# Matmuls of z for two groups at once in a two-layer hybrid encoder

## What is computed

```
proj = x @ w_in[i]                 # GLU input | two branch gates | z (2048) | xBC (4096) | dt
A:  u = a * sigmoid(gt); u = depthwise_conv(u, 31 taps); u = silu(layer_norm(u)); y_a = u @ w_a_out
B:  xbc = silu(depthwise_conv(xBC, 5 taps)) -> xs (2048), B, C (8 groups of 128 each)
    y = ssd_forward + ssd_backward + xs * d_skip          # chunks of 128 tokens
    y = y * silu(z); y = y / rms(y within a group of 256) * norm_g; y_b = y @ w_b_out
merged = sigmoid(gate_A) * y_a + sigmoid(gate_B) * y_b
h  = layer_norm(alpha * x + merged @ w_o)
h2 = layer_norm(alpha * h + swiglu(h))
x  = h2 + rms_norm(p @ w_ple) * sigmoid(h2 @ w_ple_gate)
```

## Time and profile before

| | |
|---|---|
| runs | 2437.61, 2442.34 (median), 2445.15 us |
| profiled execution | 2438.85 us, span of its trace 2437.2 us |
| granted clock of TensorE | 0.996 of full speed |
| DMA moved | 406 MB, mean 167 GB/s |
| chain that ended last | PE 84%, ACT 4%, DVE 4%, DMA 3%, issue 3% |

### The profile page before, as it was taken

How to read it: one execution, slowest core, us unless ns; L and a number is a source line. 1 busy time by engine, 2 the same in 40 slices (tenths; PEclk the granted TensorE clock), 3 DMA queues, 4 the chain that set the end, 5 groups by cost and what they waited for, 6 DMA issues and landing times.

```text
span 2437.2 us, 35277 instructions
## 1 busy us (share of the span) xinstructions
PE 2380.4 (98%) x11464; PEld 1944.8 (80%) x11464; DVE 1486.2 (61%) x2553; ACT 1370.6 (56%) x2238; POOL 585.9 (24%) x721
## 2 busy tenths in 40 slices
PE   8999999999999999999999999999999999999998
PEld 6878788887777888887778787888878778888876
DVE  5899999989546111113659989989895451111136
ACT  6755666475564644345567466665746555444455
POOL 3423333242111111111134243332411111111110
PEclk9999999999999999999999999999999999999999
DMA  8576574756787788899664756747577868888884
GB/s 214 125 171 141 132 184 112 162 139 155 173 185 186 165 194 193 188 197 201 160 160 107 183 122 157 164 115 174 119 175 171 204 150 192 191 193 189 196 206 121
DMA packets 111172, 406.04 MB, mean 167 GB/s; under 512 B 12336, under 2 KB 12336, under 8 KB 110768
## 3 DMA queue, kind: packets, MB, share of 16 engines
q0 software_dynamic: 54144, 197.16, 47.4%
q1 hardware_dynamic: 55728, 202.66, 24.2%
q10 hardware_dynamic: 1152, 4.37, 0.5%
HBM read 402.04 MB, written 2.10 MB: 166 GB/s over the span
## 4 chain that ended last, share of the span: by engine, by line
PE 84%; ACT 4%; DVE 4%; DMA 3%; issue 3%; POOL 0%; ACTq 0%; SPq 0%; POOLq 0%; DVEq 0%; another core or an unknown queue 0%
PE bank L835 22%; PE bank L837 22%; PE bank L836 22%; PE bank L878 3%; PE bank L877 3%; PE bank L880 2%; DMA w_raw<-w_stream 2%; PE bank L951 2%; PE bank L957 1%; DMA w_lo<-w_stream 1%; ACT w_lo L465 1%; PE bank L939 1%; ACT w_hi L464 1%; PE bank L1156 1%; PE bank L922 1%
## 5 line engine op out<-in xcount | busy, mean ns | idle before, releaser
L352 POOL DMA_DIRECT2D w_lo<-w_stream x376 | 327.5, 871 | 1576.4 <-ACT w_lo L465 1525.4
L835 PE MATMUL bank<-x_hi,w_hi 128*128 128x512 f32 x1728 | 685.9, 397 | 4.6 <-DMA w_lo<-w_stream 4.6
L837 PE MATMUL bank<-x_hi,w_lo 128*128 128x512 f32 x1728 | 673.8, 390 | 0.0
L836 PE MATMUL bank<-x_lo,w_hi 128*128 128x512 f32 x1728 | 672.8, 389 | 0.0
L464 ACT ACTIVATE w_hi<-w_raw 128x1024 fp32r<-128x1024 f32 x378 | 402.7, 1065 | 287.2 <-PE bank L837 232.0
L465 ACT ACTIVATE w_lo<-w_raw 128x1024 fp32r<-128x1024 f32 x378 | 399.9, 1058 | 0.0
L835 PEld LDWEIGHTS bank<-x_hi,w_hi 128*128 128x128 f32 x1728 | 324.5, 188 | 74.7 <-issue 8.8
L837 PEld LDWEIGHTS bank<-x_hi,w_lo 128*128 128x128 f32 x1728 | 324.3, 188 | 69.0
L836 PEld LDWEIGHTS bank<-x_lo,w_hi 128*128 128x128 f32 x1728 | 324.6, 188 | 68.3 <-issue 3.3
L1238 DVE SCALAR_TENSOR_TENSOR z_a<-glu_out,params,z_a 128x497 f32<-128x497 f32 (+14 forms) x480 | 320.1, 737 | 0.0
L1685 DVE TENSOR_TENSOR glu_out<-bank,sigmoids 128x512 f32<-128x512 f32 x44 | 30.4, 692 | 416.5 <-PE bank L837 416.5
(11 more groups left out here) (242 smaller groups left out, 3611.2 us busy)
## 6 DMA issues: line engine op xcount, KB each, us to landing
w_raw<-w_stream SPq DMA_DIRECT2D x378, 512.0 KB, 4.5
w_lo<-w_stream POOLq DMA_DIRECT2D x376, 512.0 KB, 7.2
z_b<-x_in SPq DMA_DIRECT2D x4, 512.0 KB, 6.9
w_ple_in<-w_ple ACTq DMA_DIRECT2D x2, 1024.0 KB, 11.4
out<-z_b SPq DMA_DIRECT2D x4, 512.0 KB, 7.1
ple_p<-p_in ACTq DMA_DIRECT2D x2, 512.0 KB, 6.7
params<-par_in ACTq DMA_DIRECT2D x2, 340.0 KB, 3.8
tmp_m<-w_dt ACTq DMA_DIRECT2D x2, 256.0 KB, 5.2
```

Of the source, the lines that this page charges most:

```text
L352: gp.dma_start(wlo[:, s, :], w_stream[cyc, s].bitcast(F32R), accum_op=ALU.add).then_inc(lo_done[s], 16)
L835: pe.matmul(dst, wh, mh, start=first, stop=False)
L836: pe.matmul(dst, wh, ml, start=False, stop=False)
L837: return pe.matmul(dst, wl, mh, start=False, stop=last)
```

## The change

TensorE makes z of both groups of a pair together: the stationary operand stays a tile of x (128 features x 128 tokens), and the moving one is now 512 columns, z's filters of both groups for one tile of features. A slot holds two such tiles, so z takes four passes over the four banks (`z_pass`, one chunk of tokens per bank), of 24 matmuls each. The filter tiles of the second group's xs, xs and B come ahead of z in the stream, and its C behind. Results of z stay in the four banks until the fourth pass; then ScalarE's `z_gate` takes each chunk. With that:

- ScalarE's roundings (`hi`) and GpSimd's `lo` issues change places within the pair, and z_gate, the squares and the takes of the convolution input with them.
- ScalarE makes the middle tap of three of the four convolution calls of a pair and of the long convolution of branch A (`middle_tap`, `middle_tap_a`, Identity with scale and bias). VectorE's `taps` leaves it out there.
- The squares for the group norm write into z_tok in place of a tile of their own.
- Gate B's second cycle: its slot 0 is rounded among the squares of branch A, and its first two tiles are copied to glu_out and taken as sigmoids later.
- Gate of PLE: a slot is rounded ahead of the sigmoid instead of behind it. The square root of PLE's norm comes after the fifth rounding of the activations instead of the eighth.

```diff
@@ TensorE: z
-            def z_tiles(cyc, s, chunks=range(CH)):
...
-                    for k in range(KT):
-                        h, l, end = whi[:, s:s + 2, w], wlo[:, s:s + 2, w], k == KT - 1
-                        pe.matmul(dst, xh[:, k, t], h, start=k == 0, stop=False)
...
+            def z_pass(c0, n, chunks=range(CH), last=True):
+                cyc, s = on(c0, 1 if n == 0 else 2), (n - 1) % SLOTS
+                pe.wait_ge(lo_done[s], 16 * (cyc[0] + 1))
+                for i, c in enumerate(chunks):
+                    if n == 0:
+                        pe.wait_ge(evac[c], seen(c0[1] + (1 if c == CH - 1 else 2)))
+                    t = slice(c * P, (c + 1) * P)
+                    for k in (2 * n, 2 * n + 1):
+                        w = slice(k % 2 * T, (k % 2 + 1) * T)
+                        pe.matmul(bank[c][:, :], xh[:, k, t], whi[:, s, w], start=k == 0, stop=False)
+                        pe.matmul(bank[c][:, :], xh[:, k, t], wlo[:, s, w], start=False, stop=False)
+                        q = pe.matmul(bank[c][:, :], xl[:, k, t], whi[:, s, w], start=False, stop=k == KT - 1)
...
@@ TensorE: pair
-                z_tiles(on(c0, 1), 0)
-                dense(on(c0, 1), 2, xh, xl)
+                for n in range(3):
+                    dense(on(c0, 1), n, xh, xl)
                 xs_transpose(G0)
                 exponent(G0, 0, True)
-                dense(on(c0, 1), 3, xh, xl)
+                z_pass(c0, 0, (3, 0, 1, 2))
                 b_transpose(G0)
                 c_dot_b(G0)
                 exponent(G0, 1, True)
-                dense(on(c0, 2), 0, xh, xl)
+                z_pass(c0, 1, (0, 1), False)
+                state(G0, 0)
                 exponent(G0, 2)
-                state(G0, 0)
-                dense(on(c0, 2), 1, xh, xl)
+                z_pass(c0, 1, (2, 3))
                 exponent(G0, 3)
                 state(G0, 1)
                 state(G0, 2)
-                z_tiles(on(c0, 2), 2, (0, 1))
+                z_pass(c0, 2)
+                z_pass(c0, 3, (0, 1), False)
                 y_chunk(G0, 0)
-                z_tiles(on(c0, 2), 2, (2,))
+                z_pass(c0, 3, (2,), False)
                 y_chunk(G0, 1)
                 y_chunk(G0, 2)
-                z_tiles(on(c0, 2), 2, (3,))
+                z_pass(c0, 3, (3,))
+                dense(on(c0, 2), 3, xh, xl, ks=low)
                 y_chunk(G0, 3)
+                dense(on(c0, 2), 3, xh, xl, ks=high)
@@ ScalarE
+            def middle_tap(g, c, of_):
+                act.activation(feat[:, c, :], of_, ACT.Identity, scale=group_par(g, c * TAPS + TAPS // 2),
+                               bias=group_par(g, 4 * TAPS + c)).then_inc(mid_done, 1)
...
+            def z_gate(pair_, c0, c):
...
+                if c < CH - 1:
+                    act.wait_ge(z_done, seen((CH - 1) * pair_ + c + 1))
+                else:
+                    act.wait_ge(used[2], seen(c0[1] + 3))
+                act.activation(ztok[:, c, :, :].rearrange("p q e -> p (q e)"), bank[c][:, :], ACT.Silu).then_inc(evac[c], 1)
...
+                squares_a(L, range(5))
+                hi(on(post, C_GATE_B + 1), 0)
+                squares_a(L, range(5, KT))
...
                 for s in range(SLOTS):
                     gate_b(0, s)
-                    hi(on(post, C_GATE_B + 1), s)
+                    if s < SLOTS - 1:
+                        hi(on(post, C_GATE_B + 1), s + 1)
...
+                    if m in (5, 7):
+                        act.wait_ge(sqa_used, seen(KT * (L + 1)))
+                        take(on(post, C_GATE_B + 1), (m - 5) // 2, u[:, (m - 5) // 2, :])
                 for s in range(SLOTS):
-                    gate_b(1, s)
+                    gate_kept(s) if s < 2 else gate_b(1, s)
...
@@ VectorE: pair
-                    mask_cb(G0)
-                    conv(g1, G1, 0, [(c0 + 1, 2), (c0 + 1, 3)])
+                    conv(g1, G1, 0, [(c0 + 1, 0), (c0 + 1, 1)], m0 + 6)
+                    mask_cb(G0)
...
-                    conv(g1, G1, 2, [(c0 + 2, 0), (c0 + 2, 1)])
+                    conv(g1, G1, 2, [(c0 + 1, 2), (c0 + 2, 3)])
```

More of the change, by code:

```diff
@@ L97 @@
 Y_BANKS = (6, 4)
+MIDS = 8
 def on(cyc, n):
@@ L637, in pair @@
                 for c in range(CH):
-                    square(G0, c)
-                z_gates(G1, on(c0, 2), (2, 3))
+                    z_gate(L * PAIRS + j, c0, c)
+                square(0, G0, 0)
+                square(0, G0, 1)
+                hi(on(c0, 3), 2)
+                square(0, G0, 2)
+                square(0, G0, 3)
+                take(on(c0, 2), 3, cin[:, 3, :])
+                hi(on(c0, 3), 3)
                 xs_tokens(G1, 0)
@@ L865, in projection @@
                     i.then_inc(used[b], 1)
[L867 to L883 removed]
+            def z_pass(c0, n, chunks=range(CH), last=True):
[10 more added lines that the diff above has]
+                        q = pe.matmul(bank[c][:, :], xl[:, k, t], whi[:, s, w], start=False, stop=k == KT - 1)
+                    if last and i == len(chunks) - 1:
+                        q.then_inc(used[s], 1)
+                    elif n == SLOTS - 1:
+                        q.then_inc(z_done, 1)
             def xs_transpose(G):
@@ L1225, in heads, with taps @@
                 return t.rearrange("p (h e) -> p h e", h=HG)
-            def taps(outs, ins, ws, count, finish, between=lambda n: None):
+            def taps(outs, ins, ws, count, finish, between=lambda n: None, mid_made=False):
                 mid = count // 2
@@ L1236, in taps @@
                             continue
-                        dve.wait_ge(dve_order, issued(0 if n == count - 1 and i else 1))
+                        if n > 1 or not mid_made:
+                            dve.wait_ge(dve_order, issued(0 if n == count - 1 and i else 1))
                         q = dve.scalar_tensor_tensor(out=outs[i][:, a:b], in0=ins[i][:, a + o:b + o], scalar=w[:, k:k + 1],
```

152 lines of the change are left out of this document (87 added, 65 removed).

## The result

The changed kernel takes 2444.89 us in the median of 20 runs (2442.80 to 2455.23); the kernel before, in 20 runs beside it, 2437.24 (2430.44 to 2446.74). The ratio is 1.0033, with a 95% interval of 1.0023 to 1.0043: slower by a third of a per cent. Forecast was 2441 and no difference that can be told, -1.2 us against the kernel before. That 2441 lies 4 us from the measured time is luck: it was built on 2442.34, the median of three runs of the kernel before, and the median of twenty is 2437.24. The difference is +7.7, nine above the forecast one, so the terms matter more than the sum.

A forecast was written before the change was run, and what follows sets the result against it. The prediction took the kernel to be bound by TensorE's matmul pace and a few waits on its in-order queue. Pairs +4.0, gate stage -1.0 and gate of PLE -4.2 sum to -1.2 us: 2441 us, range 2434 to 2447, with rivals 2427 to 2452.

The forecast's parts named there:

- the list of waits that come: New TensorE waits in a pair: 1.6 us before exponents 2 and 3, 0.9 at bank 3, pair's end unchanged.
- the wait of the transposes on Silu: In a pair, TensorE's wait before the transposes of xs, released by ScalarE's Silu, goes: 0.61 us a pair gained.
- z: z matmuls in a pair: 96 of 512 columns at 0.2267 us replace 194 of 256 or fewer, saving 1.38 us.
- Exponents 2 and 3: First group of a pair: TensorE waits for GpSimd's operands, 0.6 us before exponent 2 and 1.0 before 3, together 1.6.
- Bank 3: After the last z chunk, dense slot 3 waits for ScalarE's gate copy of the same bank: 0.9 us a pair.
- tmp_y: End of the pair: TensorE's wait on VectorE's chain stays as it was, 1.4 us a pair.
- Gate stage: Outside the pairs: 1.5 us gained in layer 1, 0.5 lost in layer 2, sum -1.0 us.
- Gate of PLE: Outside the pairs: low halves go out earlier, waits of 1.94 and 2.24 us go, -4.2 us over both layers.
- the pair's +0.5: Forecast sum of a pair's terms: -1.38 - 0.61 + 1.6 + 0.9 us, times eight +4.
- The faster one (GpSimd in time): Rival in the pairs: GpSimd's operands in time or nearly, -0.7 to 0 us a pair, 2430 us in all; chance 0.30.
- The slow clock: Rival in the pairs: idle time drops TensorE's clock to half, +13 us over eight pairs, 2454 in all; chance 0.13.
- z at 0.233: Rival for the z matmuls: w_hi streams as slowly as y_hi, the saving halves, +5 us, 2446 in all; chance 0.10.

The follow-up runs named there:

- e2: Changed kernel with GpSimd making the operand of a first group's exponent 0 at the end of the pair before, in pairs 2 to 4 of each layer: 2433.34 us.
- e5: Changed kernel with VectorE pausing before a pair's first convolution call until the four selects of exponent 0 are done: 2432.35 us.
- e1: Changed kernel with VectorE again making the middle taps of the first group's first convolution call: 2450.34 us, 146.7 us a pair.
- e10: Changed kernel with those middle taps back on VectorE and the operand of exponent 0 one weight issue earlier in GpSimd's queue: 2436.68 us, 144.2 a pair.
- e11: Changed kernel with only the operand of exponent 0 one weight issue earlier in GpSimd's queue, taps left on ScalarE: 2503.9 us in one run.
- e13: Changed kernel with the operand of exponent 0 made in the pair before and the last two z chunks together ahead of y_chunks 1 and 2: 2426.07 us.
- e6: Changed kernel with each z matmul of 512 columns split into two of 256 in the same places: 2453.40 us, ratio 1.0045 to the kernel before.
- e7: Changed kernel with operand of exponent 0 early, y_chunk 3 ahead of the dense block of slot 3, states 1 and 2 ahead of exponent 3: 2438.42 us.
- e12: Changed kernel with exponent 0's operand early, states 1 and 2 before exponent 3, last two z chunks together before y_chunks 1 and 2: 2418.13 us, ratio 0.9905.

## Why the prediction was wrong

**The step that failed** is the list of waits that come. It begins at exponent 1 and takes for granted that the operand of exponent 0 is there; the prediction forecast only that the wait of the transposes on Silu goes, 0.61 us. It did go, and exponent 0, right behind the transposes, waits 1.9 us in six pairs: +11.4 us, which e2 and e5 give back (11.6 and 12.5, good to some 3 us). The price of a select was taken from the earlier trace rows, 2.9 to 3.8 us for four. The row that speaks was in the trace of before and not read, the 3.60 us for two selects at 333.20. The prediction did price VectorE's taps against GpSimd's selects, but only at exponents 2 and 3. And the middle taps were priced on the engine that gets them (ScalarE, idle time) and on the one that loses them (VectorE, less work), not for the engine that got in beside them (GpSimd). That is half of it: the new order also brings the select 1.1 us nearer to the place of the tap (1.06 us ahead of it in e1, 2.2 in the kernel before), and in the changed kernel only tap and earlier place together let it in (e1, e10, e11).

Term by term, per pair unless said otherwise:

- z: forecast -1.38, measured -0.65 (its pieces, each from its first start to the start of what follows and without idle time, sum to 23.46 us after and 24.11 before). The pace was nearly right, 0.229 instead of 0.2267, which is 0.25 of the missing 0.73. Another 0.32 is the run-out of the last z matmul ahead of two waits (exponent 3 and bank 3), 0.16 each; the waits by pace below hold it too. The long first matmul of a piece (0.63 from 371.24 to 371.87) isn't a cost of z; see below the list. The remaining 0.16 was not traced.
- Exponents 2 and 3: forecast 1.6. Measured 0.74 - 0.24 = 0.5 and 1.36 - 0.23 = 1.13, together 1.63. Right.
- Bank 3: forecast 0.9. Measured 0.86 idle, 1.02 by pace; from e2 to e13 a pair falls from 144.2 to 143.1. Right.
- tmp_y: forecast unchanged at 1.4. It is 0.93 in this pair (0.92 to 0.96 in six pairs, 1.3 in two), so 0.5 better. VectorE's chain and TensorE's shifted against each other by that.
- Gate stage: forecast -1.5 and +0.5. From the projection to the norm's end (568.87 to 796.00, 578.63 to 804.41) it is -1.35 in layer 1; in layer 2 (1778.69 to 2003.81, 1791.98 to 2017.68) +0.58. Right, and for the reason given: the projection's own low half.
- Gate of PLE: forecast -4.2 over both layers. Measured -3.13 (74.64 to 71.51) and -2.68 (53.44 to 50.76), -5.8. The late waits behind the two that were counted, 1.04 and 0.42 in layer 1, shrank too.
- 5.1 us of the last stretch are no effect of the change: the profiled execution of the kernel before lost them in the down stage of layer 2 (379.95 us against 374.86) at a late weight (ScalarE waits 4.52 us for w_raw up to 2367.30), behind which the granted clock was half for 6.8 us from 2372.6. Without them the two profiles would stand 11 us apart; the kernel before loses such time in some runs and not in others (2430 to 2447), and the medians stand 7.7 apart.

The z matmul at 371.24 stands 0.03 us behind the start of the last of four matmuls that make chunk states, and those come 0.43 apart (369.93, L988). From 371.21 to 371.87 it is 0.66 = 0.43 + 0.23, so nothing is lost there. The kernel before shows the same at that place, 0.54 from 369.52 to 370.06 = 0.43 + 0.12:

```profile
369.54 0.68 PE L877 MATMUL bank<-w_hi,x_hi 128*128 128x256 f32 x1
370.06 0.28 PE L878 MATMUL bank<-w_lo,x_hi 128*128 128x256 f32 x1
```

Behind the states and behind two y_chunks this puts 1.0 us into both sums of z (24.11 - 23.14 before; 1.0 of 23.46 - 96 x 0.2267 = 1.7 after). That edges between z and small blocks ate half of the saving, the theory with which e6 was run, doesn't hold.

With exponent 0 (+1.9 in six pairs) and z as it was (+0.7) added, the pair's +0.5 becomes 3.1, less 0.5 for tmp_y 2.6; the time lines give 2.8, and what lies between (0.2, or 0.5 if z's run-out is counted once) was not traced. That the forecast's own sum lies near the measured time is luck of two kinds: the base was 5 us too high, and the gain at PLE was larger than said.

**The rivals.** The faster one (GpSimd in time) was the wrong way round: GpSimd was later than any case considered. The slow clock did not appear in the pairs of the changed kernel, but the mechanism is real, as e7 shows. z at 0.233 did not happen.

## What to carry to other kernels

Before moving an instruction off an engine, look who ran beside it: a different kind of instruction, or a gap, in a long run of two-input VectorE instructions can be the moment at which GpSimd gets to its data. Putting it back may not be enough once the order has moved (e1). A GpSimd duration far above its usual one, in the trace that you already have (3.60 for two against 1.27), is a warning with a place and a time. And take covers away, or add them, only with the other engine's clock in hand: three edits worth 24 us alone gave 6 together (e7), and 27 when one of them was replaced so that the small blocks stood where VectorE had time (e12).
